# Start of a fused transformer block: sum of squares on two engines, fp32 products for a narrow projection, a second weight load queued directly, small loads moved back

## The reference

```python
def rms_norm(x, g):
    y = xf * lax.rsqrt(jnp.mean(xf * xf, axis=-1, keepdims=True) + RMS_EPS)
    return (y * g).astype(x.dtype)
...
h = rms_norm(x, norm_mix[l])
(cb, cc, cx, aq, ak, av, gq, gk, gv, gr, gz) = jnp.split(h @ w_in[l], split_points, axis=-1)
...
log_a = jax.nn.log_sigmoid((z @ w_alpha + b_alpha)) / GLA_GATE_TEMP      # z is gz, 16 columns
```

## Time and profile before

| what | value |
|---|---|
| median of 3 runs | 711.92 us (711.28 to 712.20) |
| the profiled execution's own time | 712.9 us |
| its span in the profile | 711.1 us |
| PE busy | 587.2 us (83%) |
| DMA | 247.73 MB, mean 348 GB/s |

### The profile page before, as it was taken

The page is one execution under the profiler, slowest core; times in us unless marked ns, Lnnn a source line. Parts: engine busy times, 40 slices in busy tenths (PEclk is TensorE's granted clock), DMA queues, the critical chain, the costliest instruction groups (busy, mean ns, idle before and its releaser), DMA issues.

```text
span 711.1 us, 15452 instructions
## 1 busy us (share of the span) xinstructions
PE 587.2 (83%) x6636; PEld 410.9 (58%) x6636; DVE 302.8 (43%) x626; ACT 189.7 (27%) x332; POOL 29.6 (4%) x56
## 2 busy tenths in 40 slices
PE   8999999999999999996875767776678656887584
PEld 5787899999999885553432333333334333443342
DVE  6475976985474945442222222122312222111412
ACT  4493355473535434110111001010011100110111
POOL 8003000000000020000000000000000000000000
PEclk9999999999999999998798788797877988687969
DMA  8995546536579699999999999999999999999993
GB/s 253 349 328 187 163 137 203 175 121 213 175 274 420 234 395 369 427 425 428 425 427 425 426 429 427 426 427 427 425 425 428 427 427 427 424 426 427 423 417 146
DMA packets 39619, 247.73 MB, mean 348 GB/s; under 512 B 4360, under 2 KB 6496, under 8 KB 25472
## 3 DMA queue, kind: packets, MB, share of 16 engines
q1 hardware_dynamic: 38096, 245.44, 85.6%
q0 software_dynamic: 912, 1.25, 1.0%
q10 hardware_dynamic: 544, 0.06, 0.1%
HBM read 245.67 MB, written 1.06 MB: 347 GB/s over the span
## 4 chain that ended last, share of the span: by engine, by line
PE 50%; DMA 44%; SPq 1%; another core or an unknown queue 1%; DVE 1%; issue 1%; ACT 0%; ACTq 0%; DVEq 0%
DMA wide<-in_w_expert_up 38%; PE ps L1366 8%; PE ps L1029 6%; PE ps L1030 6%; PE ps L1031 6%; DMA wide<-in_w_expert_down 3%; PE ps L1401 3%; PE ps L1002 3%; PE ps L1004 3%; PE ps L1003 3%; PE ps L1325 2%; DMA ring<-in_w_in 2%; PE ps L1413 1%; PE ps L1381 1%; SPq L526 1%
## 5 line engine op out<-in xcount | busy, mean ns | idle before, releaser
L1366 PE MATMUL ps<-wide,xe 128*32 128x256 f32 x2048 | 162.1, 470 | 109.3 <-DMA wide<-in_w_expert_up 109.3
L1366 PEld LDWEIGHTS ps<-wide,xe 128*32 128x32 f32 x2048 | 75.9, 131 | 176.9 <-issue 132.1
L1882 DVE TENSOR_TENSOR xe<-ps,g_ffn 128x256 f32<-128x256 f32 x32 | 13.6, 425 | 258.4 <-PE ps L1334 258.4
L1486 DVE TENSOR_TENSOR ring_lo<-ring,w_hi 128x1024 fp32r<-128x1024 f32 x76 | 92.0, 1228 | 46.2 <-ACT w_hi L721 45.7
L721 ACT ACTIVATE w_hi<-ring 128x1024 fp32r<-128x1024 f32 x76 | 79.0, 1058 | 58.8 <-PE ps L1031 35.3
L1029 PE MATMUL ps<-hT_hi,w_hi 128*128 128x256 f32 x320 | 89.4, 279 | 0.2 <-DVE hT_lo L1498 0.2
L1030 PE MATMUL ps<-hT_lo,w_hi 128*128 128x256 f32 x320 | 88.4, 276 | 0.0
L1031 PE MATMUL ps<-hT_hi,ring_lo 128*128 128x256 f32 x320 | 88.4, 276 | 0.0
L925 ACT ACTIVATE he<-ps 128x128 f32<-128x128 f32 x32 | 8.9, 278 | 207.7 <-PE ps L1381 204.7
L1401 PE MATMUL ps<-wide,he 128*32 128x256 f32 x1024 | 62.5, 382 | 1.9 <-DMA wide<-in_w_expert_down 1.8
L1029 PEld LDWEIGHTS ps<-hT_hi,w_hi 128*128 128x128 f32 x320 | 60.1, 188 | 0.7 <-issue 0.7
(11 more groups left out here) (276 smaller groups left out, 785.9 us busy)
## 6 DMA issues: line engine op xcount, KB each, us to landing
wide<-in_w_expert_gate SPq DMA_DIRECT2D x27, 2048.0 KB, 45.6
wide<-in_w_expert_up SPq DMA_DIRECT2D x27, 2048.0 KB, 48.2
wide<-in_w_expert_down SPq DMA_DIRECT2D x27, 2048.0 KB, 41.1
ring<-in_w_in SPq DMA_DIRECT2D x8, 2048.0 KB, 16.1
ring<-in_w_merge_gate SPq DMA_DIRECT2D x6, 2048.0 KB, 9.6
wide<-in_w_expert_gate SPq DMA_DIRECT2D x10, 1024.0 KB, 13.2
wide<-in_w_expert_up SPq DMA_DIRECT2D x10, 1024.0 KB, 10.6
wide<-in_w_expert_down SPq DMA_DIRECT2D x9, 1024.0 KB, 11.8
```

What stands on the lines that cost most here:

```text
L1366: ins = t_.matmul(ps[q * WIN:(q + 1) * WIN, b, 0:QW], xe[b][:, k % 2, k // 2, :], w, start=(k == 0), stop=(k == KD - 1))
L1486: v.tensor_tensor(piece(ring_lo, g, c), piece(ring, g, c), by_row(out_hi[g == 19][c]).bitcast(F32), ALU.subtract).then_inc(wpre_lo, 1)
```

## The change

- **Norm.** DVE sums the squares of the first half, ACT those of the second (`Square` with an accumulator). ACT takes the two square roots one after the other, behind an extra one on a constant that loads the table early. DVE scales in four pieces: features whose index modulo 8 is below 4 for both halves of x, then the rest. The transposes wait for the piece that they read.
- **z.** `w_z` stays fp32, padded to 32 columns. 16 fp32 products run in four column groups of PE (32 columns each), group q taking features `k = 4j + q` and writing PSUM partitions 32q to 32q + 31. `zT` has 128 rows, and `w_al` is repeated in four row groups, so that the next product adds the four partial sums. The splitting of `w_z` on ACT and DVE is gone. POOL zeroes the padding.
- **Loads.** SP issues unit 1 directly behind unit 0, then `w_al` four times, then unit 2. `w_z` goes on ACT's queue as its second transfer. POOL's 15 small loads wait for unit 1 to have landed.
- **Warm-up.** 14 products in place of 20.
- **Places.** Tiles of 1 KB and more start at multiples of 256 bytes, smaller ones at multiples of 64.

```diff
-N_WARM = 20
+N_WARM = 14
...
+    def fitting(at, size):
+        step = 256 if size >= 1024 else 64
+        return (at + step - 1) // step * step
...
-        off = top[0] if at is None else at
+        off = fitting(top[0], size) if at is None else at
...
                 elif g:
                     sp.dma_start(ring[s][:, :].rearrange("p (k n) -> p k n", n=n), src).then_inc(landed[s], 16)
+                    if g == 1:
+                        sp.wait_ge(sbd_zero, 1)
+                        for q in range(NQ):
+                            sp.dma_start(w_al[WIN * q:WIN * q + 16, :], w_gla_alpha[0]).then_inc(alpha_in, 16)
...
-                    sp.wait_ge(early_in, 16 * N_EARLY)
-                    sp.dma_start(w_z[:, :, :], w_in_v[:, :, 4608:4624]).then_inc(wz_in, 16)
...
+            g.memset(w_z[:, :, 16:WIN], 0.0)
+            g.memset(w_al[:, :], 0.0).then_inc(sbd_zero, 1)
...
+            pool.wait_ge(landed[1], 16)
             for dst, src in smalls:
                 pool.dma_start(dst, src).then_inc(small_in, 16)
...
-            act.dma_start(w_al[:, :], w_gla_alpha[0]).then_inc(alpha_in, 16)
+            act.dma_start(w_z[:, :, 0:16], w_in_v[:, :, 4608:4624]).then_inc(wz_in, 16)
...
-            act.wait_ge(ms_ready, 2)
-            s_.activation(stat[:, 2:4], stat[:, 0:2], ACT.Sqrt).then_inc(rms_ready, 1)
+            act.wait_ge(consts, 1)
+            s_.activation(stat[:, 63:64], ident[:, 0:1], ACT.Sqrt)
+            act.wait_ge(x_in[1], 16)
+            s_.activation(xn[:, 1, :], x_tok[:, 1, :], ACT.Square, accum_out=stat[:, 1:2]).then_inc(x_sq, 1)
+            for tt in range(TT):
+                act.wait_ge(ms_ready, tt + 1)
+                s_.activation(stat[:, 2 + tt:3 + tt], stat[:, 6 + tt:7 + tt], ACT.Sqrt).then_inc(rms_ready, 1)
...
-            act.wait_ge(wz_in, 16)
-            s_.activation(w_z_hi[:, :, :], w_z[:, :, :], ACT.Copy).then_inc(wz_hi_ready, 1)
...
-            pe.wait_ge(wz_lo_ready, 1)
-            for k in range(KD):
-                o = ps[0:16, 4, 0:T]
-                t_.matmul(o, w_z_hi[:, k, :], hT_hi[:, k, :], start=(k == 0), stop=False)
-                t_.matmul(o, w_z_hi[:, k, :], hT_lo[:, k, :], start=False, stop=False)
-                ins = t_.matmul(o, w_z_lo[:, k, :], hT_hi[:, k, :], start=False, stop=(k == KD - 1))
+            pe.wait_ge(wz_in, 16)
+            pe.wait_ge(sbd_zero, 1)
+            for j in range(KD // NQ):
+                for h in (hT_hi, hT_lo):
+                    last = j == KD // NQ - 1 and h is hT_lo
+                    for q in range(NQ):
+                        k = NQ * j + q
+                        ins = t_.matmul(ps[WIN * q:WIN * (q + 1), 4, 0:T], w_z[:, k, :], h[:, k, :].bitcast(F32),
+                                        start=(j == 0 and h is hT_hi), stop=last)
...
+            def norm_apply(tt, ks):
+                if ks[0] == 0:
+                    dve.wait_ge(rms_ready, tt + 1)
+                    link(v.reciprocal(stat[:, 4 + tt:5 + tt], stat[:, 2 + tt:3 + tt]))
+                half = slice(ks[0], ks[-1] + 1)
+                v.tensor_scalar(xn[:, tt, :].rearrange("p (f k) -> p f k", k=KD)[:, :, half],
+                                x_tok[:, tt, :].rearrange("p (f k) -> p f k", k=KD)[:, :, half], stat[:, 4 + tt:5 + tt], None,
+                                ALU.mult).then_inc(xn_ready, 1)
...
+            norm_stats(0)
+            norm_stats(1)
+            norm_apply(0, range(0, 4))
+            norm_apply(1, range(0, 4))
+            norm_apply(0, range(4, KD))
+            norm_apply(1, range(4, KD))
```

More of the change, by code:

```diff
@@ L153, in hybrid_block @@
         on_w = place("on_w", [P, 1], F32)
[L154 to L157, removed]
+        w_al_at = top[0] = fitting(top[0], 1024)
+        w_al = place("w_al", [P, 256], F32)
+        zT = place("zT", [P, T], F32)
         table = place("table", [BUCKETS, NH], F32)
[L160 to L163, removed]
+        w_z_at = top[0] = fitting(top[0], 1024)
+        top[0] += 1024
         w_r = place("w_r", [P, KD, NLOG], F32)
@@ L195, in hybrid_block @@
         npass = place("npass", [1, 1], I32)
-        region = top[0]
+        region = fitting(top[0], 1024)
         def here(name, shape, dt):
-            nonlocal_at = here_at[0]
-            here_at[0] += (int(np.prod(shape[1:])) * mybir.dt.size(dt) + 31) // 32 * 32
-            return place(name, shape, dt, at=nonlocal_at)
+            size = int(np.prod(shape[1:])) * mybir.dt.size(dt)
+            off = fitting(here_at[0], size)
+            here_at[0] = off + size
+            return place(name, shape, dt, at=off)
         here_at = [region]
-        sig0_at = here_at[0]
+        sig0_at = here_at[0] = fitting(here_at[0], 1024)
         sig0 = here("sig0", [P, KD, T], F32)
@@ L228, in hybrid_block @@
         gqk = here("gqk", [P, 4, T], F32)
-        att_at = here_at[0]
+        att_at = here_at[0] = fitting(here_at[0], 1024)
         attm = here("attm", [P, 8, P], F32)
-        gv_at = here_at[0]
+        gv_at = here_at[0] = fitting(here_at[0], 1024)
         out_hi = [w_hi, [place(f"out_hi{c}", [P, CW], F32R, at=gv_at + 4 * CW * c) for c in range(CHUNKS)]]
         gv = here("gv", [P, TT, C], F32)
-        gr_at = here_at[0]
+        gr_at = here_at[0] = fitting(here_at[0], 1024)
         gr = here("gr", [P, TT, C], F32)
         kdn = here("kdn", [P, TT, 256], F32)
-        sbd_at = here_at[0]
+        sbd_at = here_at[0] = fitting(here_at[0], 1024)
         sbd = here("sbd", [P, 3, 2, 256], F32)
-        scr_at = here_at[0]
+        scr_at = here_at[0] = fitting(here_at[0], 1024)
         scr = here("scr", [P, 2, C], F32)
+        w_z = place("w_z", [P, KD, WIN], F32, at=scr_at)
         la, e_pos, e_neg, e_rest = (qTz[:, 2 * i:2 * i + 2, :] for i in range(4))
@@ L315, in hybrid_block @@
         rms_ready = sem("rms_ready")
+        x_sq = sem("x_sq")
         xn_ready = sem("xn_ready")
@@ L743, in _ @@
             high_pre(1, (3,))
-            act.wait_ge(z_mm, 1)
-            s_.activation(zT[:, :], ps[0:16, 4, 0:T], ACT.Copy).then_inc(z_ready, 1)
-            act.wait_ge(alpha_in, 32)
+            act.wait_ge(z_mm, NQ)
+            s_.activation(zT[:, :], ps[:, 4, 0:T], ACT.Copy).then_inc(z_ready, 1)
+            act.wait_ge(alpha_in, 16 * (NQ + 1))
             high_pre(2, (0, 1))
@@ L1463, in link, with norm_stats @@
                 dve.wait_ge(v_chain, steps[0])
[L1465 to L1477, removed]
-                for tt in range(TT):
-                    v.tensor_scalar(dst[:, tt, :], src[:, tt, :], stat[:, 4 + tt:5 + tt], None,
-                                    ALU.mult).then_inc(signal, 1)
+            def norm_stats(tt):
+                if tt == 0:
+                    dve.wait_ge(x_in[0], 16)
+                    link(v.tensor_tensor_reduce(xn[:, 0, :], x_tok[:, 0, :], x_tok[:, 0, :], 1.0, 0.0, ALU.mult,
+                                                ALU.add, stat[:, 0:1]))
+                else:
+                    dve.wait_ge(x_sq, 1)
+                v.tensor_scalar(stat[:, 6 + tt:7 + tt], stat[:, tt:tt + 1], 1.0 / D, EPS, ALU.mult,
+                                ALU.add).then_inc(ms_ready, 1)
+            def norm_apply(tt, ks):
[6 more added lines that the diff above has]
+                                ALU.mult).then_inc(xn_ready, 1)
             def low_pre(g, cs=range(CHUNKS)):
@@ L1487, in low_pre @@
                                     ALU.subtract).then_inc(wpre_lo, 1)
-            norm_stats(x_tok, [xn[:, tt, :] for tt in range(TT)], ms_ready)
-            norm_apply(x_tok, xn, rms_ready, xn_ready)
+            norm_stats(0)
[4 more added lines that the diff above has]
+            norm_apply(1, range(4, KD))
             dve.wait_ge(consts, 5)
```

46 lines of the change are left out of this document (21 added, 25 removed).

## The result

| | before | after |
|---|---|---|
| median of 20 runs each, us | 712.40 | 713.29 |
| profiled execution, us (span) | 712.9 (711.1) | 712.99 (711.3) |
| ratio after / before | | 1.0015, 95% from 1.0008 to 1.0022 |
| first expert product (`wide`, `xe`), us | 271.40 | 275.81 |
| from there to the end of the span, us | 439.7 | 435.5 |

The changed kernel is about 1 us slower (0.9 in medians). That lies inside the 0.2% that I called no change, but the forecast was 710.0 and the range ended at 712.2: the prediction was wrong. The last two lines of the table say where to look. PE comes to the experts 4.4 us later, and the expert stage then gives 4.2 us back. The row of after from which the first of them is read (timeline of PE), and its slices of GB/s, which answer to the earlier trace rows: the stream comes to its full rate a slice later and then stands a little higher.

The account below looks back on a forecast made before the run. The expert weight stream was taken as the bound, its start set by PE ahead of unit 1. Gains 0.66 + 0.9 + 0.3 = 1.9 us gave 711.0 for the profiled execution, 710.0 as median; range 708.4 to 712.2.

Parts of the forecast that it names:

- Places: Tile starts on multiples of 256: no row tells what a DMA pays for other starts, so counted as nothing.
- PE never rests from unit 0 on: PE from 11 to 272 us: longest waits 0.7 and 0.5 us, so time gained ahead of unit 1 starts the expert stream earlier.
- the signs that I listed: Checks on unit 0, z, unit 1, PE waits, x_tok, first expert load (1.9 us earlier) and stream (426 GB/s; 428 means wrong).
- Aligned writes: Rival in the expert stream: rate nears 429 GB/s, 2.9 us at most, half taken, 708.5 us; chance 0.08.
- Norm: Ahead of unit 0: scalings from 7.7, first product at 11.35 instead of 11.66 us, gain 0.3.
- my best bound: Norm, if all 0.7 us of the earlier transposes reached PE: first product at 10.95, gain 0.7.
- z: Between units 0 and 1: 16 fp32 products take 1.86 us instead of 2.74, gain 0.9 (bounds 0.8 and 1.0).
- Unit 1 directly behind unit 0: SP's queue: unit 1 issued at 3.8 instead of 10.52, lands near 18, PE's wait ahead of it goes, gain 0.66 us.
- the step that I had costed at nothing on the gain side: POOL's 15 small loads begin near 18 us, slowing units 2 to 4, hidden by PE's work; cost nothing.
- Warm-up: Start of PE: fourteen products instead of 20 end near 8.7 us, cost nothing if PE reaches 2.4 GHz by then.
- doubling: DVE's strided norm scalings take 0.48 us each; rival without it: 0.6 apart, unit 0 at 12.2, 710.8 us, chance 0.10.
- late clock: Rival: after 14 warm-up products unit 0 may begin at 1.2 GHz, products at 0.23 us; chance 0.13, of which 0.05 slower.

Follow-up runs that it names:

- e1: Changed kernel with every tile back at its place of before, so the head's edits alone; 709.45 us, ratio 0.995 to the kernel before.
- e2: Kernel before with only the changed kernel's places; 714.99 us, ratio 1.0033 to the kernel before.
- e6: Changed kernel with hT, branch tiles and eight expert places at 192 modulo 256, rings on multiples of 256; 706.31 us, ratio 0.9909.
- e5: e1 with every place rounded to 64 bytes instead of 32, hT kept at 64 modulo 256; 709.21 us, ratio 0.9949.
- e3: Changed kernel with hT, branch tiles and eight expert places 64 bytes further on, rings on multiples of 256; 711.49 us, ratio 0.9987.
- e7: e1 with z computed as before the change (split w_z, 24 products of 16 columns) and w_al loaded once; 710.27 us, ratio 0.997.
- e8: e1 with w_z loaded on SP between units 0 and 1, behind the wait for the two early loads; 710.42 us, ratio 0.9967.
- e9: e1 with the 15 small loads issued at once instead of behind unit 1's landing; 709.88 us, ratio 0.9974.
- e4: Changed kernel with rings, converted weights and x at 128 modulo 256, hT and region on multiples of 256; 714.39 us, ratio 1.0019.

## Why the prediction was wrong, step by step

- **Places ("I take nothing").** This step failed. I looked for a price only where a DMA writes and left PE's operands out. Their distance went from 192 to 0, and `feat` from 0.34 to 0.36 us for three products: 7.2 us at the first expert product (275.81 against e1's 268.59). The same edit gave back 3 to 4 us in the expert stage (3.8 in these two executions, 435.5 against 439.3; 3.4 by the medians). Net, the places cost 3.8 us in medians on top of the head's edits (713.29 against 709.45) and 2.6 without them (e2).
- **"PE never rests from unit 0 on", so a gain passes through.** It was true, and it misled me: no wait can appear, but a busy engine can slow down. Of the signs that I listed, two answered to the places: the first load of expert weights, forecast 1.9 us earlier, was issued 2.3 later (207.77 against 205.46, timeline of SP), and the stream stood above 428. None of them looked at the pace of the products behind unit 0.
- **Aligned writes, the rival at 708.5.** The mechanism was there. The rate is the one that I called its most, 429 GB/s against 426, and it was worth about 3 us, near the 2.9 that I had at most: e6 beats e5, of its own group, by 2.9 in medians and e1 by 3.1, and PE comes to the experts at 268.61, 269.08 and 268.59 in the three. The single executions of the table show 3.8 to 4.5 less in the expert stage (e1 to after, before to e2); the rate does not explain the last 1 us or so of that. The Trainium skill, "DMA: Bandwidth & Descriptors", under "How a descriptor splits into AXI transactions", speaks of reads, and my estimate from it was 0.4 to 0.8%; the stream is 0.7% faster here. The table's runs with the rings (14 of 22 places) on multiples of 256 take 435.2 to 435.9 us for the expert stage, those with only the region there 436.6 and 437.1, those with neither 438.1 to 440.3. The loads of the units, in pieces of 2 KB where the experts' are of 16 KB, show it more strongly: from 34 to 46 us they move 382 to 388 GB/s where the rings stand 64 or 128 past a multiple of 256, and 402 to 408 where they stand on one (after, e2, e3, e6). No wait of PE hung on these.
- **Norm, 0.3.** The mechanism was right, the size low: unit 0 began at 11.02 and not 11.35, a gain of 0.64, near my best bound of 0.7. The scalings started at 7.48, not 7.7, and `w_z` did not hold up x, which landed at 5.98 (before, DVE began on it at 5.94). But the 0.64 is of one pair of executions: unit 0 begins at 10.88 to 11.41 in the eleven kernels with the new head, and at 11.66 and 11.97 in the two with the old one.
- **z, 0.9.** Right for z itself: 1.86 us, 32 rows. I put nothing at the product behind it, "in the same passes"; with 128 rows it gave another 0.4 (e7 against e1).
- **Unit 1 directly behind unit 0, 0.66.** The wait went, and e1's first product of unit 1 stands at 24.52, where I had 24.8. The cause was misplaced: e8 and e9 show that putting off the small loads did it, the step that I had costed at nothing on the gain side.
- **Warm-up, doubling.** Right: scalings of 0.49 us, and no product of unit 0 at the pace of 0.23 that a late clock would have meant. In e5 the 14 products took 5.85 us (5.21 in after), nearly the 6.0 of the lower level, and unit 0 still took 11.1 us, as in e1.
- **What the sum lacked.** e1 gains 2.13 us at unit 1, 2.6 by 48 us and 2.8 at the experts. Of the 0.5 in between, 0.4 is the product of `zT` and `w_al`, inside unit 1. The last 0.2 are 48 products of `feat` from 105.93 on, which the kernel before ran at 0.120 us each and e1 at 0.116.

What stays open: why the distance matters. PE and PEld are both busy for all of the 40 us in those windows, so the weights of one product are loaded while another runs. The 512-column products of `tok`, in which the weights' chunks move and `hT` stands, follow another pattern: 15 of them near 80 us take 3.43 us before, 3.40 after, but 3.50 in e3 and 3.49 in e4. And the same distance also had two paces: 0.34 or 0.35 us for three in e3, in e6's unit 0, and in the 48 products of before and e7 named above. So the distance decides what pace is usual, and something else, perhaps when a unit begins, can choose another. The Trainium skill, "SBUF — State Buffer", under "SBUF: two separate sides", names one shared port pair as the only contention among engines and says that PE never waits on anyone. By that rule the products would keep their pace wherever their operands lie, and e2 would have had 352 of them in the window, not 336; which access waits no run here shows.

## What to carry to other kernels

Before aligning everything, list which engine reads each tile together with which other tile: here a round number for both operands of a product cost 7 us, and the distance that the old layout had was worth keeping. Count instructions in windows of a stretch in which the engine is always busy; a slower pace leaves no wait, and shares and chains don't show it. When one transfer is late, ask what runs beside it as well as what stands ahead of it.

## What the runs showed of the hardware that I had not expected

- Back-to-back fp32r products with 128 x 128 weights and 256 moving columns start every 0.113 us where the moving operand lies 192 bytes beyond the weights modulo 256, and every 0.120 us where both start on a multiple of 256 (352 and 336 products in 40 us), at the same granted clock; 64 and 128 bytes gave 0.118 to 0.120. A few stretches kept another pace than their distance's.
- Expert weights that land on multiples of 256 bytes, in pieces of 16 KB, stream at 429 GB/s, others at 426. Loads in pieces of 2 KB move 402 to 408 against 382 to 388.
- Two fp32 products with 128 rows of weights, in between products of full width, took 0.4 us less than the same two with 16 rows (e1 against e7).
- 15 small loads from POOL's queue hold the bandwidth at 209 to 212 GB/s for 5 us (e9, before), in which 365 to 386 are to be had without them (e1, e8, after).
